# Two transformer blocks on one core: the maps of the forgetting attention turned by transfers and VectorE, lambda by VectorE alone, factor matmuls moved in the third feed-forward

## The reference, cut to what matters

```
def forgetting_attention(q, k, v, logf):          # 8 heads of width 64
    c = jnp.cumsum(logf, axis=1).transpose(0, 2, 1)
    for s0 in range(0, s_len, Q_BLOCK):           # blocks of 128 queries
        logits = q[:, s0:s1] @ k[:, :s1] * scale + c[queries] - c[keys]
        p = softmax(where(kpos <= qpos, logits, -inf))
        outs.append(p @ v[:, :s1])

lam = exp(sum(lambda_q1 * lambda_k1)) - exp(sum(lambda_q2 * lambda_k2)) + lam_init

def swiglu_2(h, w1, w3, w2):
    return (jax.nn.silu(h @ w1) * (h @ w3)) @ w2  # hidden width 2816
```

## Time and profile before

| | |
|---|---|
| median of three runs | 957.12 us |
| profiled execution, own time | 956.9 us |
| its span, first to last instruction | 955.2 us |
| TensorE matmul busy | 947.0 us (99%), 5102 instructions |
| VectorE busy | 699.3 us (73%) |
| ScalarE busy | 507.7 us (53%) |
| GpSimd busy | 18.8 us (2%) |
| chain that ended last, TensorE's share | 98% |
| granted TensorE clock, mean | 0.999 of full |
| SP's queue, share of 16 DMA engines | 57.3% |

### The profile page before, as it was taken

The page is one execution under the profiler, slowest core; times in us unless marked ns, Lnnn a source line. Parts: engine busy times, 40 slices in busy tenths (PEclk is TensorE's granted clock), DMA queues, the critical chain, the costliest instruction groups (busy, mean ns, idle before and its releaser), DMA issues.

```text
span 955.2 us, 13264 instructions
## 1 busy us (share of the span) xinstructions
PE 947.0 (99%) x5102; PEld 817.6 (86%) x5102; DVE 699.3 (73%) x749; ACT 507.7 (53%) x695; POOL 18.8 (2%) x24
## 2 busy tenths in 40 slices
PE   9999999999999999999999999999999999999997
PEld 8888888888888888888888888898888888888886
DVE  6889768687767577877677686594776587677676
ACT  6535767664434345634343446574878554343443
POOL 0000000050000000000000000000000000000000
PEclk9999999999999999999999999999999999999999
DMA  9754694775565667564646554734545446646551
GB/s 310 238 188 153 218 272 174 199 264 176 187 208 176 220 171 246 175 201 151 213 164 208 187 184 166 227 114 170 177 141 189 133 133 203 213 158 215 179 176 45
DMA packets 147204, 179.54 MB, mean 188 GB/s; under 512 B 34315, under 2 KB 114653, under 8 KB 147037
## 3 DMA queue, kind: packets, MB, share of 16 engines
q1 hardware_dynamic: 144476, 176.38, 57.3%
q10 hardware_dynamic: 2688, 2.63, 0.8%
HBM read 175.32 MB, written 1.05 MB: 185 GB/s over the span
## 4 chain that ended last, share of the span: by engine, by line
PE 98%; DVE 1%; ACT 0%; issue 0%; DVEq 0%; ACTq 0%
PE up_banks L845 13%; PE gate_banks L845 12%; PE bank L568 9%; PE bank L569 9%; PE bank L570 9%; PE up_banks L568 7%; PE up_banks L569 7%; PE up_banks L570 7%; PE gate_banks L850 7%; PE up_banks L850 6%; PE up_banks L693 2%; PE up_banks L696 1%; PE bank L751 1%; PE bank L996 0%; PE gate_banks L646 0%; PE bank L646 0%
## 5 line engine op out<-in xcount | busy, mean ns | idle before, releaser
L1288 ACT ACTIVATE w_hi<-stage 128x2048 fp32r<-128x2048 f32 x81 | 154.5, 1907 | 171.5 <-PE gate_banks L850 171.5
L1870 DVE TENSOR_TENSOR w_lo<-stage,w_hi 128x2048 fp32r<-128x2048 f32 x76 | 173.6, 2287 | 53.1 <-ACT w_hi L1281 52.5
L1876 DVE TENSOR_TENSOR w_lo<-stage,w_hi 128x2048 fp32r<-128x2048 f32 x81 | 185.4, 2289 | 10.8 <-ACT w_hi L1288 10.8
L1281 ACT ACTIVATE w_hi<-stage 128x2048 fp32r<-128x2048 f32 x77 | 147.2, 1913 | 55.9 <-PE bank L570 20.5
L845 PE MATMUL gate_banks<-act_both,w_hi 128*128 128x512 f32 x528 | 129.0, 390 | 0.0
L845 PE MATMUL up_banks<-act_both,w_hi 128*128 128x512 f32 x528 | 125.3, 389 | 1.1 <-DVE gate L2011 1.1
L1990 DVE TENSOR_REDUCE gate<-gate_banks 128x512 f32<-128x1024 f32 x33 | 40.4, 1224 | 110.3 <-PE gate_banks L850 110.3
L845 PEld LDWEIGHTS up_banks<-act_both,w_hi 128*128 128x128 f32 x528 | 98.6, 188 | 21.7 <-issue 1.5
L845 PEld LDWEIGHTS gate_banks<-act_both,w_hi 128*128 128x128 f32 x528 | 97.3, 188 | 19.0 <-DVE w_lo L1870 0.2
L568 PE MATMUL bank<-w_hi,ffn_hi 128*128 128x512 f32 x240 | 93.8, 391 | 0.0
L569 PE MATMUL bank<-w_lo,ffn_hi 128*128 128x512 f32 x240 | 93.7, 391 | 0.0
(11 more groups left out here) (418 smaller groups left out, 1464.7 us busy)
## 6 DMA issues: line engine op xcount, KB each, us to landing
stage<-in_ffn_w SPq DMA_DIRECT2D x66, 1024.0 KB, 5.3
stage<-in_w_in SPq DMA_DIRECT2D x31, 1024.0 KB, 5.3
stage<-in_w_gate_up SPq DMA_DIRECT2D x22, 1024.0 KB, 5.1
stage<-in_w_down SPq DMA_DIRECT2D x11, 1024.0 KB, 4.9
stage<-in_w_out SPq DMA_DIRECT2D x8, 1024.0 KB, 5.5
stage<-in_mem_w_kv SPq DMA_DIRECT2D x8, 1024.0 KB, 5.1
stage<-in_w_branch SPq DMA_DIRECT2D x4, 1024.0 KB, 5.5
stage<-in_mem_w_q SPq DMA_DIRECT2D x4, 1024.0 KB, 5.0
```

What stands on the lines that cost most here:

```text
L1281: act.activation(w_hi[:, place, :], stage[:, place, :], copy).then_inc(hi_done, 1)
L1288: act.activation(w_hi[:, place, :], stage[:, place, :], copy).then_inc(hi_done, 1)
L1870: dve.tensor_tensor(w_lo[:, place, :], stage[:, place, :], w_hi[:, place, :].bitcast(F32), ALU.subtract).then_inc(lo_done, 1)
L1876: dve.tensor_tensor(w_lo[:, place, :], stage[:, place, :], w_hi[:, place, :].bitcast(F32), ALU.subtract).then_inc(lo_done, 1)
```

## The change

The maps: SP's queue carries 16 transfers for each tile that place 32x32 blocks of L0 and L1 at their transposed position (`p_blocks`), into `forget` and `table`. VectorE turns each block, 512 columns at a time (`turn_blocks`, two instructions for tile 0 and four for tile 1, semaphore `p_turned`), into the spaces of `k_T` (`p_a`) and `q_pad` (`p_b`). The transposes of these maps on TensorE and their copies on ScalarE go. Chunks 17 to 20 are issued between the groups of transfers. The value matmuls have three pieces of 128 queries by 128 keys for each head in place of one of 256 and one of 128 columns, and stand behind the first half product of the last gate pair. VectorE's list and ScalarE's are reordered around it: the convolution blocks 1 to 3 are each one chunk later, ScalarE's loads of the memory and of `table` wait for the pieces of tile 1 and the turned maps. Between chunks 25 and 28 VectorE does `lo(26)` and the second half of the merged gates before it turns the memory.

Lambda: the four vectors are loaded broadcast over 128 partitions, VectorE multiplies and reduces along the row, and ScalarE takes the exponential behind the first tile's.

Third feed-forward: the factor matmuls run between the two halves of the high matmuls of the up product, in place of behind the second of its low ones.

```diff
+        def p_blocks(engine, tile, pieces):
+            L, to = ((L0, p_blocks0), (L1, p_blocks1))[tile]
+            from_ = L[:, :, :].rearrange("p a b -> p (a b)").rearrange("p (m k) -> p m k", k=P)
+            to = to.rearrange("p (m q) -> p m q", q=P)
+            for i in pieces:
+                q, r = slice(32 * (i // 4), 32 * (i // 4) + 32), slice(32 * (i % 4), 32 * (i % 4) + 32)
+                engine.dma_start(to[r, :, q], from_[q, :, r]).then_inc(p_landed[tile], 16)
...
-            for p in range(4):
-                token_pair(GATE_C + 2 * p, w_in, 3080 + 512 * p)
+            for c in range(GATE_C, GATE_A + 1):
+                gate_weights(c)
+            sp.wait_ge(negc_ready, 1)
+            sp.wait_ge(p_done, 1)
+            p_blocks(sp, 0, range(4))
+            gate_weights(GATE_A + 1)
+            p_blocks(sp, 0, range(4, 7))
+            gate_weights(GATE_A + 2)
+            p_blocks(sp, 0, range(7, 16))
+            gate_weights(GATE_A + 3)
+            sp.wait_ge(sel_done, 1)
+            sp.wait_ge(p_done, 2)
+            p_blocks(sp, 1, range(16))
+            first_branch_weights()
...
                     for m in range(2):
                         for k in range(KD):
+                            if second is not None and m == 1 and k == 0:
+                                second()
                             high(m, k)
                     for m in range(2):
                         for k in range(KD):
-                            if late_rows is not None and m == 0 and k == 2:
-                                late_rows()
                             mm = low(m, k)
...
-            pe.wait_ge(lg_free, 8)
-            for e in range(2):
-                turn_probs(e, 0, lambda m: L0[:, m, :], 4 * e, 0)
-            pe.wait_ge(par_ready, 2)
-            pe.matmul(bank[SUM][:, 0:2], ones, lam_p, start=True, stop=True).then_inc(lam_done, 1)
             up_tok(GATE_C + 2, act_hi, act_lo, 1)
-            for e in range(2, 6):
-                k0 = P * ((e - 2) // 2)
-                turn_probs(e, 1, lambda m: L1[:, m, k0:k0 + P], 4 * (e % 2), 0)
             up_tok(GATE_A, act_hi, act_lo, 0)
             up_tok(GATE_A, act_hi, act_lo, 1)
-            pe.wait_ge(tp_free, 6)
+            up_tok(GATE_A + 2, act_hi, act_lo, 0)
+            pe.wait_ge(lg_free, 8)
+            pe.wait_ge(p_turned, 6)
             for b in range(4):
...
-                    pe.matmul(pair[ACC + b][own[i], 0, :], v_tok[:, 0, vs[i]], p_T0[:, 2 * b + i, :],
+                    pe.matmul(pair[ACC + b][own[i], 0, 0:P], v_tok[:, 0, vs[i]], p_a[:, 2 * b + i, :], start=True, stop=True)
+                for i in range(2):
+                    pe.matmul(pair[ACC + b][own[i], 0, P:T], v_tok[:, 0, vs[i]], p_b[:, 4 * b + 2 * i, :],
...
-            up_tok(GATE_A + 2, act_hi, act_lo, 0)
             up_tok(GATE_A + 2, act_hi, act_lo, 1)
...
+            gate_in(GATE_C, 1, 0)
             conv_hi(0)
-            for e in range(2):
-                keep_probs(e, p_T0[:, 4 * e:4 * e + 4, 0:P])
...
+            hi(18)
             conv_hi(1)
-            hi(18)
+            hi(19)
+            gate_in(GATE_A, 0, 0)
             conv_hi(2)
-            conv_hi(3)
-            act.wait_ge(tp_done, 6)
+            gate_in(GATE_A, 0, 1)
+            act.wait_ge(p_landed[1], 16 * 16)
             act.dma_start(mem_nat, a["mem_2"][0].rearrange("(t p) d -> p t d", p=P)).then_inc(mem_landed, 16)
-            act.wait_ge(lg_done, 8)
+            act.wait_ge(p_turned, 6)
...
-            hi(19)
-            gate_in(GATE_A, 0, 0)
-            gate_in(GATE_A, 0, 1)
+            conv_hi(3)
             hi(20)
...
             lo(6)
+            dve.wait_ge(lam_landed, 16 * 4)
+            then(dve.tensor_tensor(lam_rows[:, 0:2, :], lam_rows[:, 0:2, :], lam_rows[:, 2:4, :], ALU.mult))
+            dve.tensor_reduce(lam_p, lam_rows[:, 0:2, :], AX, ALU.add).then_inc(par_ready, 1)
...
             normal(1, L1, T)
+            lo(17)
...
+            def turn_blocks(tile, of, to, n):
+                dve.wait_ge(p_landed[tile], 16 * 16)
+                for i in range(n):
+                    dve.transpose(to[:, 512 * i:512 * i + 512], of[:, 512 * i:512 * i + 512]).then_inc(p_turned, 1)
...
+            turn_blocks(0, p_blocks0, pa_flat, 2)
             conv_lo(0)
             conv(1)
-            lo(17)
+            lo(18)
+            conv_lo(1)
+            conv(2)
+            lo(19)
+            turn_blocks(1, p_blocks1, pb_flat, 4)
+            conv_lo(2)
+            conv(3)
             dve.wait_ge(lamx_done, 1)
...
             lo(25)
+            lo(26)
+            merged_lo(1)
             dve.wait_ge(blocks_landed, 16 * 32)
```

More of the change, by code:

```diff
@@ L160, in build @@
         idle = L0[:, 0, :]
+        lam_rows = L1[:, 0, :].rearrange("p (a n) -> p a n", a=4)
+        p_blocks0 = forget[:, :, :].rearrange("p a b -> p (a b)")
+        p_blocks1 = table[:, :, :].rearrange("p a b -> p (a b)")
+        pa_flat, pb_flat = k_T[:, :, :].rearrange("p a b -> p (a b)"), q_pad[:, :, :, :].rearrange("p a b t -> p (a b t)")
+        p_a, p_b = (x.rearrange("p (m q) -> p m q", q=P) for x in (pa_flat, pb_flat))
         gain_rows = k_T[:, :, :].rearrange("p a b -> p (a b)")
@@ L259, in build @@
         x_turned, x_done = sem("x_turned"), sem("x_done")
+        lam_landed = sem("lam_landed")
+        p_landed, p_turned = [sem(f"p_landed{i}") for i in range(2)], sem("p_turned")
         x_blocks_landed, x_blocks_turned = sem("x_blocks_landed"), sem("x_blocks_turned")
@@ L488, in _ @@
             for i in range(4):
-                rows(BR0 + i, a["w_branch"][0, i % 2], 0, 4, 512 * (i // 2), 512, slot(BR0 + i))
+                if i:
+                    rows(BR0 + i, a["w_branch"][0, i % 2], 0, 4, 512 * (i // 2), 512, slot(BR0 + i))
                 if i == 1:
@@ L851, in low_part, with halves_product @@
                                  start=False, stop=k == KD - 1, skip_group_check=True)
-            def halves_product(banks, place, ready=None, base=0, between=None, late_rows=None):
+            def halves_product(banks, place, ready=None, base=0, between=None, second=None):
                 def high(m, k):
@@ L1113, in _ @@
             pe.wait_ge(lg_free, 16)
-            turn_probs(6, 2, lambda m: L0[:, 2 * m, :], 0, 6)
-            for e in (7, 8):
-                k0 = P * (e - 7)
-                turn_probs(e, 3, lambda m: L1[:, 2 * m, k0:k0 + P], 0, 6)
+            turn_probs(0, 2, lambda m: L0[:, 2 * m, :], 0)
+            for e in (1, 2):
+                k0 = P * (e - 1)
+                turn_probs(e, 3, lambda m: L1[:, 2 * m, k0:k0 + P], 0)
             up(RK + 1, act_hi, act_lo)
             wait_read(pe, DV + 1)
-            pe.wait_ge(tp_free, 9)
+            pe.wait_ge(tp_free, 3)
             for t in range(2):
@@ L1536, in key_read @@
                 act.activation(raw_k[:, t, 512 * p:512 * p + 512], src, copy).then_inc(up_free_act, 1)
+            for i in range(4, KD):
+                merged_hi(i)
             for b in range(KD):
-                if b == 4:
-                    for i in range(4, KD):
-                        merged_hi(i)
                 act.wait_ge(memt_turned, b // 2 + 1)
```

65 lines of the change are left out of this document (24 added, 41 removed).

## The result

The changed kernel takes 959.16 us (nine runs, 957.59 to 960.65) against 956.79 for the kernel before on the same chip: ratio 1.0025, 95% interval 1.0017 to 1.0034. It is slower by 2.4 us, where 2.0 us less was forecast, and it lies outside the range of 952.7 to 957.9. The profiled execution took 960.3 us, span 958.6, against 956.9 and 955.2: 3.4 us more, so it is one of the slower ones of its nine. The difference is followed in this execution.

What follows compares the result with a forecast made beforehand. The prediction took TensorE's instruction queue as the bound. From the profiled execution's 956.9 us it took 1.4 (feed-forward) and 0.6 (arriving relief) to get 954.9, so it forecast a median of 955.1, range 952.7 to 957.9.

Steps and rivals of the forecast that it cites:

- the one that decides: SP's memory blocks behind y_done 4: 18.6 us from 119.8, chunk 24 issued at 138.4, output product starting at 152.5.
- rival (b): Weight train as slow as today, 20.2 us, or tile 1 landing late: 956.2 to 957.9, no change; chance 0.24.
- 0 taken, 0.4 the bound: Behind the output product's start: chunk 27 ready within 0.3 us of its need, priced at 0, bound 0.4.
- TensorE's relief of 2.8: Map transposes and lambda matmul off TensorE: 2.8 us less work, of which 0.5 to 0.6 was to arrive.
- The third feed-forward, 1.2 of 1.4: Factor matmuls moved earlier in the up product: the stall behind line 2011 goes, gain 1.4 us, bounds 0 and 1.4.
- Lambda at 0: Lambda on VectorE with broadcast loads near the start: priced at 0, bounds -0.2 and +0.5.
- `y_done` 4 at 119.8: VectorE's fourth convolution block, ending at 113.55 today, comes 6.2 us later, at 119.8; SP's memory blocks wait for it.
- ScalarE's 5.9: Time from chunk 24's landing to ScalarE's merged halves (w_hi, table load, four squares): 5.9 us, as today.
- the wait at the merged transposes: Sign at line 1050: TensorE waits about 0.5 us there, ended by chunk 24's chain.
- The pieces of tile 1: 16 SP transfers of 64 KB at 0.745 us apiece: last issued at 112.2, landed at 114.8, transposes starting at 115.2.
- Rival (c): Tile 1 pieces hold SP's queue at up to 1.34 us each: 963.3, slower once past 1.06; chance 0.11.
- rival (a): All covers hold and the full relief arrives, -1.4 - 2.8: 952.9; needs chunk 24 landed 2.3 us sooner; chance 0.20.

Runs made afterwards that it cites:

- e5: Changed kernel with VectorE's conv_lo(2) and fourth convolution block (conv(3)) ahead of the transposes of tile 1; 960.75 us, ratio 1.0036 to the kernel before.
- e6: Changed kernel with ScalarE's two 1 MB loads moved later, the memory behind hi(21) and table behind hi(24); 958.90 us, ratio 1.0019 to the kernel before.
- e7: Changed kernel with chunk 20 issued between the eighth and ninth of the 16 pieces of tile 1; 959.16 us, ratio 1.0026 to the kernel before.
- e3: Changed kernel with the gain rows and chunk 24 ahead of the third set of memory blocks in SP's list; 956.21 us, ratio 0.9995 to the kernel before.
- e2: Changed kernel with nine idle identity matmuls ahead of TensorE's wait for the first output product; 958.21 us, ratio 1.0015 to the kernel before.
- e9: e4 with two of four memory-block calls moved behind chunk 25 and the last two one chunk further; 954.26 us, ratio 0.9971 to the kernel before.
- e13: e9 with VectorE's low part of chunk 32 moved ahead of the transposes of x; 953.32 us, ratio 0.9963 to the kernel before.
- e1: Kernel before with only the third feed-forward's factor matmuls moved; 955.59 us, ratio 0.9987 to the kernel before.
- e8: e1 plus lambda by broadcast loads and VectorE product and sum, without its matmul, maps staying on TensorE; 955.65 us, ratio 0.9988 to the kernel before.
- e12: Changed kernel with ScalarE's copies of the first four merged blocks ahead of the table load and memory squares; 958.05 us, ratio 1.0012 to the kernel before.
- e10: Changed kernel with the last 4 of the 16 pieces of tile 1 issued by ScalarE; 957.73 us, ratio 1.0003 to the kernel before.
- e4: Changed kernel with SP sending chunks 20 to 22 ahead of the first 8 memory loads, then 23 and 24, 16 loads before 25; 957.20 us, ratio 1.0001.

## Why the prediction was wrong

**The step that failed** is the term called the one that decides: "I take 18.6, since those loads have mostly drained at 119.8: chunk 24 is issued at 138.4." It took 20.4 us (120.0 to 140.4), 0.2 more than today's 20.2 of the earlier trace rows. The prediction had the times of four 1 MB loads at hand: chunk 20 at 112.8, with 21 right behind it in SP's list, and ScalarE's loads behind the landing of the pieces and behind their transposes, 115.2 and 117.7 by its own times. It did not add them up. Of ScalarE's two it took that they "have mostly drained at 119.8", though by these times the last was 2.1 us old there, and in the kernel before it landed 8.1 us after its issue. As an estimate, 4.2 MB at the 409 GB/s that the kernel before reaches at 116 to 119 us need over 10 us from 112.8 on, until 123. In the changed kernel's trace chunk 20 was in flight until 119.3, the memory until 124.4, chunk 21 until 125.8 and `table` until 128.9, and SP's issues paid for it: 6.15 + 2.50 for what takes 5.12 + 0.60 on a free queue, 2.9 us. e5 showed that the queue and not `y_done` 4 is the limit, e6 and e7 that the loads are its cause, e3 that most of the loss hangs on chunk 24's issue. The prediction had written down the price, 20.2, as its bound and as rival (b), and chose against it. That price alone gives 956.8 by its own sum, within its range. The measured 959.16 lies outside because of what follows.

**Two terms were not in the sum.** The clock: a wait of 2.2 us at the output product was forecast as 1.5 to 2, priced as its own length; half-clock matmuls added 1.7 in the profiled execution, and keeping the clock up gave back 1.0 in the medians (e2). And the first feed-forward, which the prediction did not look at (it stopped at chunk 27 with "0 taken, 0.4 the bound"): the gate product waits 0.9 because SP's pieces of x took 1.2 us longer; in the kernel before the low part was ready only 0.1 us ahead of TensorE. The product at 154.9 instead of 152.5 (2.4), the clock (1.7) and the gate product (0.9) make 5.0 of the 5.4 us between the 954.9 forecast for a profiled execution and the 960.3 of this one; the feed-forward's gain was 0.2 short.

**Right:** TensorE's relief of 2.8: the output product of e9 starts 2.83 us earlier than before. In the time, 3.68 - 1.24 = 2.4 us of it arrive (e13 against e1, each against the kernel before; e13 has one instruction of VectorE moved besides). The cutting of the value matmuls at no cost. The third feed-forward, 1.2 of 1.4. Lambda at 0 (e8). `y_done` 4 at 119.8, measured 120.0. The landing of chunk 24, 6.9, measured 7.2, and ScalarE's 5.9, measured 5.8. Of the signs named ahead: no wait near 780, no transposes of the maps on TensorE, the wait at the first output product (2.2), ended by chunk 24's chain.

**A bit off:** the wait at the merged transposes was 1.4, not about 0.5, with 0.6 more at a branch product, and both were ended by the chains of chunks 23 and 22, not by chunk 24's: the same held queue made these late too. The pieces of tile 1 came 0.80 apart, not 0.745, and the last was issued at 113.1 instead of 112.2; VectorE waited 0.56 for them at 115.4. TensorE's 1.7 of slack hid that, and `y_done` 4 came 0.2 later. The Trainium skill ("DMA: Bandwidth & Descriptors", Measured, HBM to SBUF), with 0.95 us for 64 KB, gave an estimate of 115.3 for that last issue; the trace does not bear it out for these pieces. Rival (c), the pieces alone holding the queue at over 1.06 us each, did not happen, although the kernel did come out slower; rival (a) needed chunk 24 sooner, and e9, which issues it at 132.5, is what it takes.

## What to carry to other kernels

A transfer that is priced by its issue time alone is priced too low: ask which other loads its place in the queue holds back, and whether they will all go out together behind it. When work leaves the bounding engine, list the next needs of that engine in order and move what feeds them ahead of what is needed later, here weight chunks ahead of memory blocks, which VectorE turns only from 164.7 us on in the changed kernel; one such reordering turned +2.4 into -2.6 us. And a wait removed upstream comes back at the next late thing, so a fix is read by when the product starts, not by the length of its wait.

## What the runs showed of the hardware

On SP's queue in the changed kernel loads of 32 KB go out 0.64 us apart from 128.75 on, and a 1 MB load takes 0.43 to 0.60 us to issue there. Behind four loads of 1 MB issued on two queues within 4.2 us, the single issue of chunk 22 took 2.5 to 3.5 us (the changed kernel, e2, e3, e12); in e5, where the four went out within 5.5 us, it took 3.1. The cost appears in whichever instruction stands there: the 8 small loads and chunk 22 took 6.15 + 2.50, 5.21 + 3.53 (e2) and 5.83 + 2.78 us (e3), 8.6 to 8.7 together each time.

After a wait at the product of 1.9 (e6), 2.2, 2.6 (e10) and 3.0 us (e5) TensorE worked at a granted clock of 0.52 to 0.91 in the three-microsecond windows around and behind the product's start; after 1.3 (e12) and also after 2.0 (e7) it stayed at 1.00. The length of the wait alone does not tell it. The changed kernel, e5, e6, e7 and e12 have shorter waits up to 15 us ahead of it. e10 has none from the first two microseconds on, and e4 none from there to its wait of 2.4 us at 167.2, and there too the clock fell, in e4 to 0.53 and 0.90: one such wait in a dense stream was enough.

SP's 12 pieces of x took 9.1 to 10.0 us from the first start to the last in every kernel that carries the pieces of the maps, and 7.5 to 8.4 us in the three that do not (before, e1, e8), although they start more than 60 us behind the last piece of the maps. One issue of the 12 was longer, 1.4 to 2.5 us against 0.7 to 1.3. I did not find the cause, and it stays open.
